# Norms and turns of q and k moved forward between the matmuls of the q and gate units, and the gate unit's chunks made earlier in the order

## What is computed

```python
h = rmsnorm(x, ln1_g)
q, k, v, u = split(h @ w_in, [1024, 1280, 1536])
q = rmsnorm(q.reshape(L, 16, 64), q_norm_g)     # per head
k = rmsnorm(k.reshape(L, 4, 64), k_norm_g)      # per head
y_attn = sliding_window_attention(q, k, v, sinks, rel_bias)   # window 128, 4 q heads per kv head
y = gelu(s5_scan(u, ...))                        # 64 groups of 16 channels, 64 complex states each
y_ssm = y * sigmoid(y @ w_glu)
mixed = concat([rmsnorm(y_attn, attn_out_g), rmsnorm(y_ssm, ssm_out_g)])
x = x + mixed @ w_out
x = x + (silu(h2 @ w_ff_gate) * (h2 @ w_ff_up)) @ w_ff_down   # h2 = rmsnorm(x, ln2_g)
```

## Time and profile before

| what | value |
|---|---|
| median of 3 runs | 3328.59 us (3328.2 to 3331.68) |
| the profiled execution's own time | 3326.39 us |
| its span | 3324.4 us, 38815 instructions |
| mean granted TensorE clock | 0.989 |
| busy share of the span | DVE 56%, ACT 44%, POOL 2% (TensorE stands in the rows below) |
| DMA | 593.19 MB, mean 178 GB/s |

### The profile page before, as it was taken

The page is one execution under the profiler, slowest core; times in us unless marked ns, Lnnn a source line. Parts: engine busy times, 40 slices in busy tenths (PEclk is TensorE's granted clock), DMA queues, the critical chain, the costliest instruction groups (busy, mean ns, idle before and its releaser), DMA issues. The chain is left out here.

```text
span 3324.4 us, 38815 instructions
## 1 busy us (share of the span) xinstructions
PE 3237.1 (97%) x15938; PEld 2671.3 (80%) x15938; DVE 1866.3 (56%) x1978; ACT 1472.2 (44%) x1757; POOL 80.8 (2%) x76
## 2 busy tenths in 40 slices
PE   8989999999999999999999999999999999999998
PEld 6877888888888778878888888878877788888886
DVE  7655655554555545665555555665655655555555
ACT  6534544444444444444444444444444544444443
POOL 1120000000000000000000000000000000000000
PEclk9999999999999999999999999999999999999999
DMA  6334555555555555555555555545455555555554
GB/s 207 113 112 116 177 184 189 191 192 193 193 188 192 179 172 189 192 177 188 189 188 192 189 191 189 189 159 178 151 165 165 176 190 188 189 188 188 187 189 150
DMA packets 185517, 593.19 MB, mean 178 GB/s; under 512 B 12491, under 2 KB 17276, under 8 KB 184828
## 3 DMA queue, kind: packets, MB, share of 16 engines
q1 hardware_dynamic: 185340, 590.70, 54.7%
HBM read 588.54 MB, written 2.12 MB: 178 GB/s over the span
## 5 line engine op out<-in xcount | busy, mean ns | idle before, releaser
L1155 DVE TENSOR_TENSOR LO<-RAW,HI 128x1024 fp32r<-128x1024 f32 (+1 forms) x1104 | 1346.3, 1222 | 1133.4 <-ACT HI L593 1131.2
L593 ACT ACTIVATE HI<-RAW 128x1024 fp32r<-128x1024 f32 (+1 forms) x1104 | 1158.9, 1052 | 1352.4 <-PE PS L2054 1344.0
L2054 PE MATMUL PS<-HI,KPA 128*128 128x512 f32 x5312 | 1476.6, 394 | 13.5 <-ACT HI L593 5.5
L2054 PEld LDWEIGHTS PS<-HI,KPA 128*128 128x128 f32 x5312 | 992.9, 189 | 224.3 <-issue 12.2
L2054 PE MATMUL PS<-HI,KPB 128*128 128x512 f32 x3392 | 935.2, 392 | 4.0 <-DVE ACC L1757 3.4
L2054 PE MATMUL PS<-LO,KPA 128*128 128x512 f32 x2656 | 828.6, 392 | 5.8 <-DVE LO L1155 5.8
L2054 PEld LDWEIGHTS PS<-HI,KPB 128*128 128x128 f32 x3392 | 631.0, 188 | 133.1 <-issue 5.3
L2054 PEld LDWEIGHTS PS<-LO,KPA 128*128 128x128 f32 x2656 | 501.0, 189 | 115.7 <-DVE LO L1155 8.7
L2054 PE MATMUL PS<-LO,KPB 128*128 128x512 f32 x1696 | 524.5, 390 | 0.8 <-DVE KPB L1193 0.8
L2054 PEld LDWEIGHTS PS<-LO,KPB 128*128 128x128 f32 x1696 | 318.6, 188 | 68.8 <-issue 1.2
L622 ACT ACTIVATE KPB<-PS 128x512 fp32r<-128x512 f32 x98 | 58.6, 599 | 181.6 <-PE PS L2114 181.6
(11 more groups left out here) (268 smaller groups left out, 1038.2 us busy)
## 6 DMA issues: line engine op xcount, KB each, us to landing
RAW<-in_w_up SPq DMA_DIRECT2D x128, 1024.0 KB, 5.0
RAW<-in_w_down SPq DMA_DIRECT2D x128, 1024.0 KB, 5.4
RAW<-in_w_qkv SPq DMA_DIRECT2D x48, 1024.0 KB, 5.2
RAW<-in_w_ff_gate SPq DMA_DIRECT2D x88, 512.0 KB, 3.8
RAW<-in_w_ff_up SPq DMA_DIRECT2D x88, 512.0 KB, 4.7
RAW<-in_w_ff_down SPq DMA_DIRECT2D x44, 1024.0 KB, 5.4
RAW<-in_w_in_ab SPq DMA_DIRECT2D x40, 1024.0 KB, 5.0
RAW<-in_w_in SPq DMA_DIRECT2D x16, 1024.0 KB, 5.3
```

The source lines that it names most:

```text
L593: e.activation(HI[:, s % NSPLIT, 0:w], RAW[:, d % NRAW, j, 0:w], ACT.Copy).then_inc(S("hi_made"), 1)
L1155: e.tensor_tensor(LO[:, h, 0:w], RAW[:, d % NRAW, j, 0:w], HI[:, h, 0:w].bitcast(F32), ALU.subtract).then_inc(S("lo_made"), 1)
L2054: ins = e.matmul(PS[:, b + j, 0:cw], l, r[:, h, 512 * j:512 * j + cw], start=(i == 0 and part == 0), stop=(last and part == 2))
```

## The change

- k: the root and the four multiplies are moved into the q unit (VectorE's side calls 14 and 15, GpSimd's 12); the two k turns stand in the second and third side call of `glu`, one in each, both in bank 5, and wait for the lane's first turn rather than for its gelu.
- q: both tiles are squared in the first side call, the second one in `LG1` as a second buffer; sums and means of both follow in the same call; there is a root for each tile (16 columns each, in GpSimd's first and second call), and the multiplies stand in the third and fifth call. The turns of q stand in the sixth and seventh.
- The last output of each lane comes one side call earlier on TensorE, and its gelu on ScalarE.
- The chunks of `glu` are made by a table, `Y_DUE`: chunk 1 before step 1, chunk 2 before step 3, chunk 3 before step 5.
- A sigmoid of one column (`WARM`) stands behind the last q copy on ScalarE.
- The first two scores stand in the last side call of `glu`, and VectorE has the first two logits behind two of the four gate products instead of all four.

```diff
--- before.py
+++ after.py
@@ -238,6 +238,9 @@
         return self.n
 
 
+Y_DUE = (1, 2, 2, 3, 3, 4, 4, 4)
+
+
 def due(i, nk, ahead):
 
     return (min(i + ahead, 2 * i + 4, nk) + 1) // 2
@@ -284,7 +287,7 @@
             next(g, None)
     made = have
     for i in range(n):
-        while feeder is not None and made < due(i, n, ahead):
+        while feeder is not None and made < (ahead[i] if isinstance(ahead, tuple) else due(i, n, ahead)):
             next(feeder)
             made += 1
         step(i, between if i < n - 1 else None)
@@ -341,8 +344,8 @@
     LAM = sb("LAM", [128, 3, 32])
     B0 = sb("B0", [128, 2, 512])
     RB, OH, WV = (sb(n, [128, w]) for n, w in (("RB", 16), ("OH", 383), ("WV", 383)))
-    ONE = sb("ONE", [128, 1])
-    KD = nc.alloc_sbuf_tensor_at("KD", [128, 2, 4, 128], F32, offset=at[0] - 64 - 2 * 1536 - 64 - 4096)
+    ONE, WARM = sb("ONE", [128, 1]), sb("WARM", [128, 1])
+    KD = nc.alloc_sbuf_tensor_at("KD", [128, 2, 4, 128], F32, offset=at[0] - 2 * 64 - 2 * 1536 - 64 - 4096)
     LG1 = sb("LG1", [128, 4, 384])
     at[0] += (kpa_at - at[0]) % 512
     kb = [at[0]]
@@ -379,6 +382,7 @@
     LG, PT = [None] * 3, [None] * 3
     LG[0], PT[0] = sb("LG0", [128, 4, 384], where=ph), sb("PT0", [128, 4, 384], where=ph)
     LG[1] = LG1
+    SQQ = [SQ[:, :], LG1[:, :, :].rearrange("p h c -> p (h c)")[:, 0:1024]]
     SQS = sb("SQS", [128, 8, 256], where=ph)
     GT = sb("GT", [128, 8, 256], where=ph)
     ph = [ph_at + 32768]
@@ -435,10 +439,10 @@
     POSTS = ("mix0", "mlp0", "mix1", "mlp1")
     PN = {n: dict(part=small(4), ss=small(2), ms=small(2), r=small(2), squared=4 * i, added=8 * i) for i, n in enumerate(POSTS)}
     PN["mix0"]["g"], PN["mlp0"]["g"], PN["mix1"]["g"], PN["mlp1"]["g"] = GPM, GPF, GPW, GPF
-    ROOTS = ("ln1", "k", "q", "S", "A", "ln2", "pre0", "vn", "mix0", "mpre0", "mlp0", "pre1", "mix1", "mpre1", "mlp1")
+    ROOTS = ("ln1", "k", "q0", "q1", "S", "A", "ln2", "pre0", "vn", "mix0", "mpre0", "mlp0", "pre1", "mix1", "mpre1", "mlp1")
     ROOT = {n: i + 1 for i, n in enumerate(ROOTS)}
     RT = {n: (NM[n]["ms"], NM[n]["r"], 2) for n in NORMS} | {n: (PN[n]["ms"], PN[n]["r"], 2) for n in POSTS}
-    RT |= {n: (small(w), small(w), w) for n, w in (("q", 32), ("k", 8), ("A", 2), ("S", 2), ("vn", 2))}
+    RT |= {n: (small(w), small(w), w) for n, w in (("q0", 16), ("q1", 16), ("k", 8), ("A", 2), ("S", 2), ("vn", 2))}
     sqs, sks, ssA, ssS, mu2, vs2 = small(32), small(8), small(2), small(2), small(2), small(2)
     HS_ST = [dict(mx=small(12), mm=small(8), ng=small(8), sm=small(8), sk=small(8), den=small(8), rc=small(8)) for _ in range(2)]
     HS_ST.append(HS_ST[0])
@@ -462,6 +466,10 @@
 
     def small3(t):
         return t[:, :].rearrange("p (j c) -> p j c", c=16)
+
+    def qk_bank(n):
+
+        return 5 if n < 2 else 4 + n % 2
 
     def lane_view(t):
 
@@ -758,7 +766,7 @@
             for _ in range(6 if p else 2):
                 yield
             for k in range(4):
-                for _ in range(3):
+                for _ in range(2 if k == 3 else 3):
                     yield
                 q.wait_ge(S(f"ssm{p}_y"), k + 1)
                 e.activation(yT[:, 2 * k + p, :], PS[:, 4 + 2 * p, 256:512], ACT.Gelu_apprx_tanh).then_inc(S(f"ssm{p}_out"), 1)
@@ -776,23 +784,25 @@
             for t in range(2):
                 q.wait_ge(S("evac_act"), U["q"].ea[t])
                 q.wait_ge(S("k_summed"), 2)
-                q.wait_ge(S("q_summed"), t)
-                e.activation(SQ[:, :], q_sb[:, t, :], ACT.Square).then_inc(S("q_squared"), 1)
-                yield
+                e.activation(SQQ[t], q_sb[:, t, :], ACT.Square).then_inc(S("q_squared"), 1)
+            yield
 
         def attn_prep():
             def out_of(n, dst, c, gain):
                 q.wait_ge(S("qk_turned"), n + 1)
-                q.wait_ge(S("ssm1_back"), 4)
-                q.wait_ge(S("ssm0_back"), 4)
-                e.activation(dst[:, c:c + 2, :].rearrange("p a b -> p (a b)"), PS[:, 4 + n % 2, :], ACT.Copy,
+                for p in range(2):
+                    q.wait_ge(S(f"ssm{p}_back"), 2 if n < 2 else 4)
+                e.activation(dst[:, c:c + 2, :].rearrange("p a b -> p (a b)"), PS[:, qk_bank(n), :], ACT.Copy,
                              scale=par(gain)).then_inc(S("qk_turned_out"), 1)
             for c in range(2):
                 out_of(c, kT, 2 * c, "kg")
+                yield
             yield
             yield
             for c in range(4):
                 out_of(2 + c, qT, 2 * c, "qg")
+                if c == 3:
+                    e.activation(WARM[:, 0:1], ONE[:, 0:1], ACT.Sigmoid)
                 if c % 2:
                     yield
 
@@ -915,8 +926,8 @@
         unit("u", None, [pr], [pr], to_sb(lambda t: u_sb[:, t, :], "ln1"))
         S0, S1, pr2 = ssm(0), ssm(1), prep2()
         unit("q", None, [pr2, S0, S1, k_norm()], (), to_sb(lambda t: q_sb[:, t, :], "ln1"))
-        att = late(attn1(), 4)
-        unit("glu", y_feed(), [S0, S1, q_norm(), att], ahead=1)
+        att = late(attn1(), 1)
+        unit("glu", y_feed(), [S0, S1, q_norm(), att], ahead=Y_DUE)
         sf = s_feed()
         for n in range(3):
             gate_open(n)
@@ -1395,28 +1406,30 @@
                                 ALU.add).then_inc(S("k_summed"), 1)
             q.wait_ge(S("k_summed"), 2)
             mean("k", sks, 64, EPS)
-            yield
-
-        def q_norm():
-            yield
-            for t in range(2):
-                q.wait_ge(S("q_squared"), t + 1)
-                e.tensor_reduce(sqs[:, 16 * t:16 * t + 16], heads(SQ[:, :], 16), X, ALU.add).then_inc(S("q_summed"), 1)
-                yield
-            q.wait_ge(S("q_summed"), 2)
-            mean("q", sqs, 64, EPS)
+            for _ in range(4):
+                yield
             q.wait_ge(S("root_made"), ROOT["k"])
             for t in range(2):
                 for dd in range(2):
                     e.tensor_tensor(KD[:, t, :, 64 * dd:64 * dd + 64], heads(kv_sb[:, t, 0:256], 4),
                                     bcast(RT["k"][1][:, 4 * t:4 * t + 4], 2, 64), ALU.mult).then_inc(S("k_normed"), 1)
-            yield
-            yield
+                yield
+
+        def q_norm():
             for t in range(2):
-                q.wait_ge(S("root_made"), ROOT["q"])
-                e.tensor_tensor(heads(q_sb[:, t, :], 16), heads(q_sb[:, t, :], 16), bcast(RT["q"][1][:, 16 * t:16 * t + 16], 2, 64),
+                q.wait_ge(S("q_squared"), t + 1)
+                e.tensor_reduce(sqs[:, 16 * t:16 * t + 16], heads(SQQ[t], 16), X, ALU.add).then_inc(S("q_summed"), 1)
+            for t in range(2):
+                q.wait_ge(S("q_summed"), t + 1)
+                mean(f"q{t}", sqs[:, 16 * t:16 * t + 16], 64, EPS)
+            yield
+            for t in range(2):
+                yield
+                if t:
+                    yield
+                q.wait_ge(S("root_made"), ROOT[f"q{t}"])
+                e.tensor_tensor(heads(q_sb[:, t, :], 16), heads(q_sb[:, t, :], 16), bcast(RT[f"q{t}"][1], 2, 64),
                                 ALU.mult).then_inc(S("q_normed"), 1)
-                yield
 
         def attn_group(w, n, b0, scale, mask, ready, sinks, write):
             P, st = f"at{w}_", HS_ST[w]
@@ -1604,15 +1617,15 @@
         S0, S1, pr2 = ssm(0), ssm(1), prep2()
         unit("q", None, [pr2, S0, S1, k_norm()])
         att, sf = late(attn1(), 4), s_feed()
-        unit("glu", y_feed(), [S0, S1, q_norm(), att], ahead=1)
+        unit("glu", y_feed(), [S0, S1, q_norm(), att], ahead=Y_DUE)
         for n in range(2):
             gate_times(n)
+        next(att)
         q.wait_ge(S("gated"), 1)
         next(sf)
         for n in range(2, 4):
             gate_times(n)
-        for _ in range(2):
-            next(att)
+        next(att)
         sS = s_stats()
         unit("ws0", sf, [sS, att], [sS], add_x(0, "S"), have=1, mids=[att])
         added("ws0")
@@ -2004,14 +2017,18 @@
         mark(pp)
         root("ln1")
         S0, S1 = ssm(0), ssm(1)
-        unit("q", [S0, S1])
-        root("k")
+
+        def k_root():
+            for _ in range(11):
+                yield
+            root("k")
+            yield
+        unit("q", [S0, S1, k_root()])
 
         def q_root():
-            for _ in range(4):
-                yield
-            root("q")
-            yield
+            for t in range(2):
+                root(f"q{t}")
+                yield
         unit("glu", [S0, S1, q_root()])
         for name in ("S", "A", "ln2", "pre0", "vn", "mix0", "mpre0", "mlp0", "pre1"):
             root(name)
@@ -2236,7 +2253,7 @@
                 yield
             for k in range(4):
                 yield
-                for i in range(2):
+                for i in range(2 if k < 3 else 1):
                     if k < 3:
                         into_state(k + 1, i)
                     yield
@@ -2245,14 +2262,17 @@
 
         def attn_prep():
             def turn(n, src):
```

(16 more changed lines are left out.)

## The result

| kernel | median (range, runs) |
|---|---|
| before | 3328.59 us (3326.14 to 3331.68, 7) |
| changed | 3317.49 us (3314.13 to 3318.92, 7) |

The ratio is 0.9966, with a 95% interval of 0.9957 to 0.9976: 8 to 14 us faster, 11.1 by the medians. The forecast was 3316.2 us. The profiled execution of the changed kernel is one of 3317.49 us.

A forecast was written before the change was run, and what follows sets the result against it. TensorE, busy for 97% of the span, bounds the kernel, so only its gaps and slow clock can give time. `ws0` comes 14.4 us earlier, 2.0 are given back: 3328.6 - 12.4 = 3316.2 us, range 3311 to 3321.8.

The forecast's parts named there:

- Chunks: Gate unit: earlier low chunks remove TensorE's gaps of 2.79, 3.31 and 2.04 us ahead of steps 2, 4 and 6.
- k into the q unit: nothing: Four k multiplies, 1.3 us per side call, and the 1.65 us root cost nothing in the q unit.
- The root of 16 columns, 2.9 us, on no path: GpSimd in the gate unit: each of q's two roots takes an estimated 2.9 us and delays nothing.
- What is late next: 0.8 us at lane 1's last output: Gate unit: TensorE stands 0.8 us before that output's second half, as GpSimd's state ends at 219.1.
- no price: Gate unit: nothing charged for VectorE and GpSimd locking each other out; by the skill's rule, up to 2.9 us per root.
- The clock at its upper level: Gate unit: with no gap of over 1 us left, TensorE was taken to run at its upper clock level.
- slow stretches stay: Rival, around the start of `ws0`: two to four slow-clock stretches give back 2.6 to 5.6 us; chance 0.15.
- Gates and logits: End of gate unit: first gate at 231.7, 11.15 us earlier; second pair of logits at 237.2, 12.4 us earlier.
- the longer switch: Sigmoid table load: another 1.38 us of drain by the skill page, making the gain 11.0 us; given 0.05 of 0.61.
- Given back: 2.0 us before the next stage: After `ws0` starts 14.4 us earlier, VectorE sets the pace, so 2.0 us go into new TensorE gaps.
- the distance to the logits: From the first gate matmul to the second pair of logits: 55.92 us before, 43.5 forecast.
- The signs: Expected in the trace: no chunk waits, one wait of about 1 us, clock 1.00, `ws0` some 14 and logits 12 us earlier.

The follow-up runs named there:

- the first profile: Profiled execution of the changed kernel from its first measurement: 3317.49 us, 46.78 us from the first gate matmul to the second pair of logits.
- the second profile: Changed kernel measured again, unaltered, on another chip: median 3313.67 us, ratio 0.9957 to the kernel before; its profiled execution took 3317.44 us.
- two halves: Only the chunk table added to the kernel before: 3324.45 us (0.9985); changed kernel with the old chunk rule, moves alone: 3325.14 us (0.9989).

## Why the prediction was right, point by point

**Chunks.** Right. All three waits went (2.79, 3.31, 2.04), step 2 stood straight behind a k turn, and without the table they come back at 2.11, 3.74 and 2.26.

**k into the q unit: nothing.** Right: from a lane output in the q unit to the first gate matmul it was 53.67 us before (140.02 to 193.69) and is 53.68 now. And more than that: by the trace the multiplies could have stayed in the gate unit, in an earlier call.

**The root of 16 columns, 2.9 us, on no path.** Right: 3.42 and 2.91 us; the first is 0.5 longer, beside VectorE's chunk at 199.17. Splitting it is worth nothing up to the logits (one root: same waits).

**What is late next: 0.8 us at lane 1's last output.** The place was right, the size was the step that failed: "GpSimd's state then ends at 219.1". I had left the additions at the 1.8 us between back-turn and state, while a split and a q multiply now run beside them, and wrote beside the Trainium skill's rule on the shared port pair (page SBUF — State Buffer, section "SBUF: two separate sides") that I gave it no price, because the root of before did not show it. The additions took 3.3 us and the wait was 2.72, 1.9 more than forecast. Keeping VectorE away gave 0.95. The rule was judged by the wrong instruction: the root of 32 columns at 218.92 left VectorE's split at its 1.21 us, the additions over 256 columns do not leave a VectorE pass alone, nor does it leave them. The sign was there before: the additions at 216.98 and 217.98 took 0.93 and 0.79 us where 0.73 is usual.

**The clock at its upper level.** In the gate unit wrong in the first profile, right in the second; the term is 2.6 us. It was the rival "slow stretches stay", at another place than I named. At the place that I did name, the start of `ws0`, the lower level came as well (1.05 at 240.74), but there TensorE still waited 1.46 us for VectorE afterwards, so that part was slack, as argued against the rival.

**Gates and logits.** From the first gate to the second pair of logits I had 5.5 us, it was 5.39; the first gate itself was 3.4 us later than forecast (235.78 less 0.70, against 231.7), which is the two terms above less the 1 us of the next paragraph but one. The load of 1.28 us had the next activation right behind it (233.43 to 234.72), and the last copies ended 0.02 us before it, so the row was right; the longer switch that the Trainium skill gives (page ScalarE: Activation LUTs, section "What ACT_TABLE_LOAD costs") is not seen. That the early load helps was never in the sum as a gain, and it does not help.

**Given back: 2.0 us before the next stage.** Right in kind: `ws0` began 10.5 us earlier (with the 0.70 taken off) and the logits 9.1, so 1.4 were given back. The waits were 2.58 (forecast 2.3), none before the second set of scores (1.1) and 1.46 behind them (2.7), since TensorE was at the lower level there and came later. In the run without the early sigmoid, where the clock stayed up at that place, they were 0.41 and 2.56. The forecast's own sum does not close here: 1.1 and 2.7, of which 0.5 stood there before, add up to 3.3 and not to 2.0, and the 1.3 between have no term.

**The sum, and the luck in it.** 12.4 forecast. By the distance to the logits 9.1 us in the first profile and 11.7 in the second, by the medians 11.1. In the second profile only 0.7 are missing, though the additions alone cost 1.8. A second error ran the other way. With VectorE kept off, where the wait is 0.95 us, nearly the forecast's 0.8, the distance is 42.43 and not 43.5: the queue of TensorE was summed 1.1 us too long. The rows were laid end to end, though a block begins before the one ahead of it has ended: q turns and a step take 3.74 us together (227.76 to 231.50) where the forecast has 4.1, a k turn 0.41 (204.91 to 205.32) where it has 0.5, a whole output 2.37 (202.54 to 204.91) where it has 2.49. So against 43.5 there stand 1.8 for the additions, 2.6 for the clock and 1.1 less for the sum: 46.8, as measured. That the median came within 1.3 us of the forecast is in part the luck of errors that offset each other.

**The signs.** No waits on chunks, and step 2 straight behind a k turn: as said. The sigmoid load before the last gate step: it stood in that step (233.43; the step runs from 232.29 to 235.3). One wait of about 1 us: it was 2.72. Granted clock 1.00 from 200 to 230: 0.89 in the first profile, 1.00 in the second. `ws0` 14 us and the logits 12 earlier: 10.5 and 9.1.

## What to carry to other kernels

When an instruction is moved into a new stretch, look at what runs beside it there: two GpSimd additions that had 0.73 us each cost 3.2, because VectorE had two passes over SBUF in that very place. Where several engines hand on to each other in strict order, undo the parts of a change one at a time before crediting any: here two halves gave 4.1 and 3.4 us and 11 together, and three of the parts gave nothing. And for a few us, compare distances between two points of the trace as well as whole times: the same wait of 2.72 us on TensorE was followed at once by a stretch at half the clock in one profile of the changed kernel and not in the other. Take more than one end point for such a distance, since what is won at the first can be gone at the second.
